# Second layer of a four-layer block on Trainium2: input projections as 256-feature jobs, halves of x summed by VectorE

## The chip, the cores and the metric

The kernel runs on one core of one Trainium2 chip. The metric is the device time of one execution in microseconds (us), median of the runs. In the profile PE is TensorE, PEld its weight loads, DVE VectorE, ACT ScalarE, POOL GpSimd, SP SyncE.

## The reference

Four layers work on x (256 tokens, 2048 features): two of one block, two of another, each with an input projection of x, a mixing part, and an output projection. The change is in the second layer (`odd_layer`), whose core is:

```
proj = rmsnorm(x, norm_g) @ w_in                       # 2048 -> 6160
xc, zc, qd, kd, vd, zd, a_pre, b_pre = split_cols(proj, OD_SIZES)
xconv = causal_dwconv(xc, conv_c_w) + conv_c_b         # 4 taps along the tokens
yc = rg_lru(xconv, gate_w, gate_b, lam) * silu(zc)
q, k, v = split(silu(causal_dwconv(concat([qd, kd, vd]), conv_d_w)), 3)
od = gated_delta_chunkwise(l2norm(q), l2norm(k), v, beta, g)
yd = rmsnorm(od, onorm_g) * silu(zd)
y = concat([yc, yd]) @ w_out
```

Each of xc, zc, qd, kd, vd, zd has 1024 features. `gated_delta_chunkwise` needs the inverse of a lower triangular matrix per head and chunk. Everything is 32-bit floating point.

## The kernel before

**Precision.** Every 32-bit operand of a large product is cut into a high and a low part. ScalarE copies a weight piece to WH (`split`, line 1066), VectorE subtracts it to get WL (line 1432), TensorE forms high times high, high times low and low times high. The transposed x of a layer stands in XHL, for each of 16 k-tiles (128 input features) the high half (256 tokens) beside the low half.

**Jobs and pieces.** The work is a list of jobs (`job_list`), one for each block of output columns, and each job is cut into pieces of 512 KB of weights (`piece_list`). There are 626 pieces; piece p is loaded by SP to a ring of 8, its high part goes to a ring of 6. Three modes: "tok" has tokens on the partitions of the result; "feat" has 512 features in four groups of 128, three products of 256 columns for each group and k-tile (lines 739 to 741), 2 k-tiles to a piece; "wide" has 256 features, 4 k-tiles to a piece, and its product with the high weights takes both halves of x at once, 512 columns (lines 720, 723), with one more of 256 columns for each group with the low weights (lines 721, 722). In wide mode the accumulator (two banks of 512 columns, two accumulators in turns) holds for each group two sums of 256 columns, and whoever reads it has to add them (`halves_of`). The third and fourth layers use wide mode for their rotated inputs, the first and second "feat".

**Order.** Every engine walks through the same pieces. At piece p it does its own part of `split` for piece p + 5, then the read-out of a job that ends with p (`evacuate`), then the steps that `plan` has put at p. `plan` is written by hand: `put(slot, step, item)`. TensorE does piece p and then the small products of the steps of p. TensorE does not start a job before the accumulator of the job before the last is read out. Semaphores alone hold the engines together, and no engine leaves its order.

**The second layer** is pieces 177 to 305. Its jobs run qd 0, kd 0, ab, vd 0, qd 1, kd 1, vd 1 (pieces 177 to 225, with 193 for ab), xc (226 to 241), zd in tok mode (242 to 257), zc (258 to 273), output. A conv job (qd, kd, vd, xc) ends with ScalarE's copy from the accumulator to `conv_ring` (line 1111, two halves of 512), GpSimd's product with the row of 1/rms (line 1955), ScalarE's scaled copy (`copied`, line 1241 or 1243), VectorE's three taps for two groups of 128 features (`taps`, line 1674, six instructions) and ScalarE's `silu` (line 1249). A zc job ends with VectorE's product of accumulator and row (line 1460); `gate_c` is ScalarE's silu (line 1360) and GpSimd's product, `split_c` the high and low part of it (lines 1366, 1859).

Beside that the plan runs the delta rule of 8 heads in two halves. For each half come `delta_a`, `delta_k`, `delta_q` (lines 937 to 950 on TensorE, 1743 to 1763 on VectorE, 1296 to 1298 on ScalarE), the triangular solve `tri` in ten parts (VectorE, lines 1770 to 1795, two columns of 15 in a part; GpSimd clears three tiles ahead of it, lines 2007 to 2009; ScalarE copies its result, line 1315), then `level_x` and `level_y` (blocks of the inverse put together by products, lines 964, 978, 981) and `solve1` to `solve4`. The first `tri` stands at pieces 213 to 224, its `level_x` at 227 and `level_y` at 229; the second at 251 to 260, its `level_x` at 263. The LRU's `scan` (lines 1848 to 1852) stands at 261 to 272.

## Time and profile before

| | |
|---|---|
| median of 3 runs | 1919.39 us (1919.13 to 1920.65) |
| profiled execution: time, span | 1919.7 us, 1917.5 us |
| PE busy | 1908.2 us, 100% of the span |
| PEld busy | 1665.5 us, 87% |
| DVE busy | 1203.8 us, 63% |
| ACT busy | 1016.9 us, 53% |
| POOL busy | 165.0 us, 9% |
| SP's weight queue, share of 16 DMA engines | 52.9% |
| granted TensorE clock, mean | 0.999 |

Busy time is an average over stages with different limits. A matmul's length in the profile takes in its run through the array, so matmuls overlap and the sum of their lengths is more than the time they hold the engine; what one costs is the distance from its start to the start of the next.

### The profile page before, as it was taken

The page shows a single profiled execution, that of the slowest core. Times are in us where ns is not written, and L with a number is a line of the kernel's source. Part 1 is how long each engine was busy: PE and PEld are TensorE (multiplying, and loading weights), DVE is VectorE, ACT ScalarE, POOL GpSimd, SP SyncE. Part 2 cuts the span into 40 slices and gives each one's busy share as a digit, 9 for nine tenths or more (in the row PEclk, how much of TensorE's full clock was granted, in tenths as well). Part 3 has the DMA queues.
Part 4 walks back from the last instruction along what each step waited for, and adds up shares of the span by engine and source line. Part 5 has one row for each costly group of instructions (what it writes and reads, how often), then busy time and mean ns, then how long its engine had stood idle before and what let it go on. Part 6 is the DMA issues. An engine that isn't in the chain of part 4 may idle for free.

```text
span 1917.5 us, 27227 instructions
## 1 busy us (share of the span) xinstructions
PE 1908.2 (100%) x10884; PEld 1665.5 (87%) x10884; DVE 1203.8 (63%) x1672; ACT 1016.9 (53%) x1582; POOL 165.0 (9%) x142
## 2 busy tenths in 40 slices
PE   9999999999999999999999999999999999999998
PEld 9988888888899999898888888888888888888886
DVE  6456554554566776787557888655565778754553
ACT  7345445664557755765543345556554344446643
POOL 0000000110002101200001111000000111100110
PEclk9999999999999999999999999999999999999999
DMA  9555555555554444444565554555555555555453
GB/s 340 177 181 176 165 187 184 173 165 187 180 175 157 156 151 143 161 155 153 181 198 191 191 176 165 180 178 164 176 185 189 187 187 171 162 186 174 161 201 132
DMA packets 95037, 340.32 MB, mean 177 GB/s; under 512 B 10704, under 2 KB 11472, under 8 KB 94784
## 3 DMA queue, kind: packets, MB, share of 16 engines
q1 hardware_dynamic: 93392, 333.76, 52.9%
q0 software_dynamic: 944, 3.61, 0.6%
q8 instruction: 87, 1.43, 0.3%
q10 hardware_dynamic: 576, 1.21, 0.2%
q14 instruction: 38, 0.31, 0.1%
HBM read 336.44 MB, written 2.10 MB: 177 GB/s over the span
## 4 chain that ended last, share of the span: by engine, by line
PE 100%; ACT 0%; DVE 0%; issue 0%
PE ACC L715 18%; PE ACC L717 18%; PE ACC L716 18%; PE ACC L723 6%; PE ACC L720 6%; PE ACC L739 6%; PE ACC L740 5%; PE ACC L741 5%; PE ACC L722 3%; PE ACC L721 3%; PE PM L842 1%; PE PM L857 1%; PE PM L895 1%; PE PM L879 1%; PE PM L880 1%; PE PM L878 1%
## 5 line engine op out<-in xcount | busy, mean ns | idle before, releaser
L1432 DVE TENSOR_TENSOR WL<-RAW,WH 128x1024 fp32r<-128x1024 f32 (+1 forms) x624 | 794.6, 1289 | 545.7 <-ACT WH L1066 544.3
L1066 ACT ACTIVATE WH<-RAW 128x1024 fp32r<-128x1024 f32 (+1 forms) x626 | 651.0, 1052 | 517.6 <-PE ACC L717 279.8
L715 PE MATMUL ACC<-WH,XHL 128*128 128x512 f32 x1024 | 407.1, 398 | 0.0
L717 PE MATMUL ACC<-WH,XHL 128*128 128x512 f32 x1024 | 399.0, 390 | 0.0
L716 PE MATMUL ACC<-WL,XHL 128*128 128x512 f32 x1024 | 398.7, 389 | 0.0
L739 PE MATMUL ACC<-XHL,WH 128*128 128x256 f32 x872 | 249.8, 287 | 0.0
L740 PE MATMUL ACC<-XHL,WH 128*128 128x256 f32 x872 | 246.6, 283 | 0.0
L741 PE MATMUL ACC<-XHL,WL 128*128 128x256 f32 x872 | 246.6, 283 | 0.0
L717 PEld LDWEIGHTS ACC<-WH,XHL 128*128 128x128 f32 x1024 | 192.2, 188 | 40.7
L716 PEld LDWEIGHTS ACC<-WL,XHL 128*128 128x128 f32 x1024 | 192.4, 188 | 38.9
L715 PEld LDWEIGHTS ACC<-WH,XHL 128*128 128x128 f32 x1024 | 192.4, 188 | 38.7
L720 PE MATMUL ACC<-XHL,WH 128*128 128x512 f32 x512 | 205.3, 401 | 0.0
L723 PE MATMUL ACC<-XHL,WH 128*128 128x512 f32 x512 | 202.5, 396 | 0.0
L739 PEld LDWEIGHTS ACC<-XHL,WH 128*128 128x128 f32 x872 | 167.2, 192 | 0.6
L740 PEld LDWEIGHTS ACC<-XHL,WH 128*128 128x128 f32 x872 | 167.2, 192 | 0.2
L741 PEld LDWEIGHTS ACC<-XHL,WL 128*128 128x128 f32 x872 | 167.2, 192 | 0.0
L722 PE MATMUL ACC<-XHL,WL 128*128 128x256 f32 x512 | 142.5, 278 | 0.0
L721 PE MATMUL ACC<-XHL,WL 128*128 128x256 f32 x512 | 142.1, 277 | 0.0
L722 PEld LDWEIGHTS ACC<-XHL,WL 128*128 128x128 f32 x512 | 96.1, 188 | 23.4
L721 PEld LDWEIGHTS ACC<-XHL,WL 128*128 128x128 f32 x512 | 96.3, 188 | 21.8
L1960 POOL TENSOR_TENSOR S<-S 128x512 f32<-128x512 f32 x32 | 66.9, 2092 | 479.6 <-DVE S L1480 479.6
L715 PE MATMUL ACC<-WH,YHB 128*128 128x512 f32 x256 | 100.9, 394 | 0.0
(365 smaller groups left out, 2428.3 us busy)
## 6 DMA issues: line engine op xcount, KB each, us to landing
RAW<-in_w SPq DMA_DIRECT2D x621, 512.0 KB, 3.3
X<-in_x SPq DMA_DIRECT2D x4, 512.0 KB, 10.0
RAW<-in_w SPq DMA_DIRECT2D x6, 256.0 KB, 4.3
Y<-in_xT SPq DMA_DIRECT2D x2, 512.0 KB, 11.2
S<-in_bias POOLq DMA_DIRECT2D x8, 128.0 KB, 2.3
S<-in_od_gate_w POOLq DMA_DIRECT2D x1, 1024.0 KB, 5.9
S<-in_final_norm POOLq DMA_DIRECT2D x1, 1024.0 KB, 7.3
out<-Y SPq DMA_DIRECT2D x2, 512.0 KB, 2.6
```

What stands on the lines that cost most here:

```text
L715: e.matmul(o, th, hi[:, kk, :], start=f, stop=False)
L716: e.matmul(o, th, lo[:, kk, :], start=False, stop=False)
L717: m = e.matmul(o, tl, hi[:, kk, :], start=False, stop=l)
L720: e.matmul(acc[0], wh0, XHL3[:, kt, :], start=f, stop=False, skip_group_check=True)
L721: e.matmul(acc[0][:, 0:256], wl0, xh, start=False, stop=l, skip_group_check=True)
L722: e.matmul(acc[1][:, 0:256], wl1, xh, start=f, stop=False, skip_group_check=True)
L723: m = e.matmul(acc[1], wh1, XHL3[:, kt, :], start=False, stop=l, skip_group_check=True)
L739: e.matmul(o, wh, xh, start=f and g % 2 == 0, stop=False, skip_group_check=True)
L740: e.matmul(o, wh, xl, start=False, stop=False, skip_group_check=True)
L741: m = e.matmul(o, wl, xh, start=False, stop=l, skip_group_check=True)
L1066: e.activation(hi, src, ACT.Copy).then_inc(s_hi)
L1432: e.tensor_tensor(lo, src, hi.bitcast(F32), ALU.subtract).then_inc(s_lo)
```

## The change

The conv jobs and the zc jobs of the second layer go from "feat" with 512 features to "wide" with 256: 8 conv jobs become 16, 2 zc jobs become 4, over the same 80 pieces. The read-out of a conv job is now one `tensor_reduce` of VectorE that adds the halves (1024 columns to 512), where ScalarE copied two times 512. That of a zc job is such a reduction and a product with the row. The plan's slots for `copied`, `taps` and `silu` follow the new jobs, one slot each behind the last piece of a job (they were spread over four slots behind the larger one). `gate_c` and `split_c` are put at new slots. The transposes `xt` of the second layer's x come one piece earlier behind an output job.

```diff
 EVAC = {...
-        "conv": (2, 0), "zc": (0, 2), "add": (0, 2), "rope": (0, 4)}
+        "conv": (0, 1), "zc": (0, 2), "add": (0, 2), "rope": (0, 4)}
...
-    def wide(layer, name, w, c0, kind):
+    def wide(layer, name, w, c0, kind, part=(0, 1, 2, 3)):
-        for i in range(4):
+        for i in part:
             jobs.append(Job(layer, name, i, w, c0 + 256 * i, 256, "wide", kind, (0, 1, 2, 3)))
...
         for name, c0 in (("qd", 2048), ("kd", 3072), ("vd", 4096)):
-            jobs.append(Job(1, name, b, w, c0 + 512 * b, 512, "feat", "conv", (0, 1, 2, 3)))
+            wide(1, name, w, c0, "conv", (2 * b, 2 * b + 1))
...
-    both(1, "xc", w, 0, "feat", "conv")
+    wide(1, "xc", w, 0, "conv")
     both(1, "zd", w, 5120, "tok", "zd")
-    both(1, "zc", w, 1024, "feat", "zc")
+    wide(1, "zc", w, 1024, "zc")
...
-                    put(L(layer, "out", q // 2) + 2, "xt", 8 * (layer + 1) + q, 1)
+                    put(L(layer, "out", q // 2) + (1 if layer == 0 else 2), "xt", 8 * (layer + 1) + q, 1)
...
-            for c in range(8):
+            for c, (name, b) in enumerate(CONV):
                 for i in range(2):
-                    put(L(1, *CONV[c]) + 1 + i, "copied", (c, i))
-                    put(L(1, *CONV[c]) + 2 + 2 * i, "taps", (c, i))
+                    last = L(1, name, 2 * b + i)
+                    put(last + 1, "copied", (c, i))
+                    put(last + 2, "taps", (c, i))
                     if c < 6:
-                        put(L(1, *CONV[c]) + 3 + 2 * i, "silu", (c, i))
+                        put(last + 3, "silu", (c, i))
...
-                    put((b1 + 92, L(1, "zc", 1) + 1)[b] + i, "gate_c", (b, i))
-                    put((b1 + 93, L(1, "zc", 1) + 2)[b] + i, "split_c", (b, i))
+                    at = L(1, "zc", 2 * b + i) + ((5, 3), (2, 1))[b][i]
+                    put(at, "gate_c", (b, i))
+                    put(at + 1 + (b == 0), "split_c", (b, i))
...
# ScalarE
-                elif J.kind == "conv":
-                    k = CONV.index((J.name, J.b))
-                    e.wait_ge(s_mm, p + 1)
-                    if k > 1:
-                        e.wait_ge(s_tap, 12 * (k - 1))
-                    for i in range(2):
-                        e.activation(conv_ring(k, i), acc[i], ACT.Copy).then_inc(s_evA)
...
# VectorE
+                elif J.kind == "conv":
+                    c, i = CONV.index((J.name, J.b // 2)), J.b % 2
+                    e.wait_ge(s_mm, p + 1)
+                    if c > 1:
+                        e.wait_ge(s_tap, 12 * c + 6 * i - 18)
+                    e.tensor_reduce(two(conv_ring(c, i)), halves_of(j), AX, ALU.add).then_inc(s_evD)
                 elif J.kind == "zc":
+                    z = two(ZC[:, 512 * (J.b % 2):512 * (J.b % 2) + 512])
                     e.wait_ge(s_mm, p + 1)
-                    if J.b:
-                        e.wait_ge(s_zg, 2)
-                    for i in range(2):
-                        e.tensor_tensor(two(ZC[:, 512 * i:512 * i + 512]), two(acc[i]), row2, ALU.mult).then_inc(s_evD)
+                    if J.b > 1:
+                        e.wait_ge(s_zg, J.b - 1)
+                    e.tensor_reduce(z, halves_of(j), AX, ALU.add).then_inc(s_evD)
+                    e.wait_ge(s_evD, D_AT[j] - 1)
+                    e.tensor_tensor(z, z, row2, ALU.mult).then_inc(s_evD)
...
# GpSimd
                 elif J.kind == "conv":
-                    k = CONV.index((J.name, J.b))
+                    x = two(conv_ring(CONV.index((J.name, J.b // 2)), J.b % 2))
                     e.wait_ge(s_row, 2)
-                    for i in range(2):
-                        x = two(conv_ring(k, i))
-                        e.wait_ge(s_evA, A_AT[j] - 1 + i)
-                        e.tensor_tensor(x, x, row2, ALU.mult).then_inc(s_cx)
+                    e.wait_ge(s_evD, D_AT[j])
+                    e.tensor_tensor(x, x, row2, ALU.mult).then_inc(s_cx)
```

Three places of the order, where the prediction has its terms. VectorE at pieces 212 and 213, the start of the first triangular solve (L1432 is the weight split, L1674 a tap, L1770 the first step of `tri`), before:

```order
L1763 SCALAR_TENSOR_TENSOR S<-PM,SM,SC 128x128
L1432 TENSOR_TENSOR WL<-RAW,WH 128x1024 x2
L1674 SCALAR_TENSOR_TENSOR S<-S,VC 128x255 x2
L1674 SCALAR_TENSOR_TENSOR S<-S,VC 128x254 x2
L1674 SCALAR_TENSOR_TENSOR S<-S,VC 128x253 x2
L1770 STREAM_TRANSPOSE SC<-SC 128x256
```

and of the change (L1427 is the weight split, L1455 the new reduction, L1677 a tap, L1773 and L1783 belong to `tri`):

```order
L1766 SCALAR_TENSOR_TENSOR S<-PM,SM,SC 128x128
L1427 TENSOR_TENSOR WL<-RAW,WH 128x1024 x2
L1455 TENSOR_REDUCE S<-ACC 128x512
L1773 STREAM_TRANSPOSE SC<-SC 128x256
L1775 TENSOR_TENSOR SC<-SC,VC 128x256
L1777 TENSOR_TENSOR SC<-SC 128x128
L1778 COPY SC<-VC 128x128
L1427 TENSOR_TENSOR WL<-RAW,WH 128x1024
L1783 STREAM_SHUFFLE SC<-SC 128x8
```

The six taps ahead of the solve have gone to piece 215, inside it, and a reduction stands in their place; two more reductions (pieces 217 and 221) stand inside the solve.

ScalarE at pieces 206 to 209 (L1066 is the weight split, L1249 `silu`, L1296 to L1298 the exponentials of `delta_a`, L1111 the conv read-out), before:

```order
L1066 ACTIVATE WH<-RAW 128x1024
L1249 ACT_TABLE_LOAD
L1249 ACTIVATE S<-S 128x256 x2
L1066 ACTIVATE WH<-RAW 128x1024
L1296 ACT_TABLE_LOAD
L1296 ACTIVATE SC<-PM,SM 128x128
L1297 ACTIVATE SC<-SC,SM 128x128
L1298 ACTIVATE SC<-SC,SM 128x128
L1066 ACTIVATE WH<-RAW 128x1024 x2
L1111 ACTIVATE S<-ACC 128x512 x2
L1296 ACTIVATE SC<-PM,SM 128x128
```

and of the change (L1068 is the weight split, L1236 `copied`, L1244 `silu`, L1291 to L1293 the exponentials):

```order
L1068 ACTIVATE WH<-RAW 128x1024
L1236 ACTIVATE S<-S,VC 128x256 x2
L1068 ACTIVATE WH<-RAW 128x1024
L1291 ACTIVATE SC<-PM,SM 128x128
L1292 ACTIVATE SC<-SC,SM 128x128
L1293 ACTIVATE SC<-SC,SM 128x128
L1068 ACTIVATE WH<-RAW 128x1024
L1244 ACT_TABLE_LOAD
L1244 ACTIVATE S<-S 128x256 x2
L1068 ACTIVATE WH<-RAW 128x1024
L1291 ACT_TABLE_LOAD
L1291 ACTIVATE SC<-PM,SM 128x128
```

The `silu` with its table load has moved from piece 206 to 208, and the exponential's table load from 207 to 209.

VectorE at pieces 260 and 261, the end of the second solve (L1789 to L1795 its last part, L1848 to L1852 a scan), before:

```order
L1789 TENSOR_TENSOR SC<-SC,VC 128x256
L1791 STREAM_TRANSPOSE SC<-SC 128x256
L1795 COPY SC<-SC 32x8x32 x4
L1432 TENSOR_TENSOR WL<-RAW,WH 128x1024
L1848 SCALAR_TENSOR_TENSOR Y<-S,Y 128x256
L1850 TENSOR_TENSOR S<-S,Y 128x256
L1852 SCALAR_TENSOR_TENSOR Y<-S 128x256
L1432 TENSOR_TENSOR WL<-RAW,WH 128x1024 x2
```

and of the change (L1461 is the reduction of the first zc job, L1463 its product with the row, L1851 to L1855 a scan):

```order
L1792 TENSOR_TENSOR SC<-SC,VC 128x256
L1794 STREAM_TRANSPOSE SC<-SC 128x256
L1798 COPY SC<-SC 32x8x32 x4
L1427 TENSOR_TENSOR WL<-RAW,WH 128x1024
L1461 TENSOR_REDUCE ZC<-ACC 128x512
L1463 TENSOR_TENSOR ZC<-ZC,C 128x512
L1851 SCALAR_TENSOR_TENSOR Y<-S,Y 128x256
L1853 TENSOR_TENSOR S<-S,Y 128x256
L1855 SCALAR_TENSOR_TENSOR Y<-S 128x256
L1427 TENSOR_TENSOR WL<-RAW,WH 128x1024 x2
```

The read-out of a zc job, which came first at piece 265, comes first at piece 261, ahead of the scan.

## Rows read from the trace of the kernel before

**Rows 1.** The page: span, busy time, granted clock by slice, chain

```profile
span 1917.5 us, 27227 instructions
PE 1908.2 (100%) x10884; PEld 1665.5 (87%) x10884; DVE 1203.8 (63%) x1672; ACT 1016.9 (53%) x1582; POOL 165.0 (9%) x142
...
PEclk9999999999999999999999999999999999999999
...
PE 100%; ACT 0%; DVE 0%; issue 0%
```

**Rows 2.** Timeline of TensorE, feature mode: start us, us, engine, line, operation

```profile
541.13 0.28 PE L739 MATMUL ACC<-XHL,WH 128*128 128x256 f32 x1
...
542.57 0.28 PE L739 MATMUL ACC<-XHL,WH 128*128 128x256 f32 x1
```

**Rows 3.** Timeline of TensorE, wide mode, third layer

```profile
1016.09 0.39 PE L720 MATMUL ACC<-XHL,WH 128*128 128x512 f32 x1
...
1016.79 0.40 PE L720 MATMUL ACC<-XHL,WH 128*128 128x512 f32 x1
```

**Rows 4.** Timeline of TensorE: first two products behind a small job, both modes

```profile
700.35 0.36 PE L739 MATMUL ACC<-XHL,WH 128*128 128x256 f32 x1
700.56 0.28 PE L740 MATMUL ACC<-XHL,WH 128*128 128x256 f32 x1
...
1105.73 0.58 PE L720 MATMUL ACC<-XHL,WH 128*128 128x512 f32 x1
1106.15 0.28 PE L721 MATMUL ACC<-XHL,WL 128*128 128x256 f32 x1
```

**Rows 5.** Four lines: count, ns shortest/median/longest, first to last start

```profile
L1472 DVE TENSOR_REDUCE S<-ACC x32: 1216/1224/1225, 1021.9 to 1673.3; 128x512 f32<-128x1024 f32 x32
L1111 ACT ACTIVATE S<-ACC x16: 582/592/598, 557.9 to 752.9; 128x512 f32<-128x512 f32 x16
L1460 DVE TENSOR_TENSOR ZC<-ACC,C x4: 680/682/691, 841.1 to 869.8; 128x512 f32<-128x512 f32 x4
L1955 POOL TENSOR_TENSOR S<-S,C x16: 1273/1298/2245, 558.7 to 754.4; 128x512 f32<-128x512 f32 x16
```

**Rows 6.** Windows of VectorE: us, busy (count), granted clock, DMA share, GB/s

```profile
650.20:692.90 42.70, 40.96 (x113) 1.00 0.52 173
833.60:880.80 47.20, 45.29 (x75) 1.00 0.45 146
```

**Rows 7.** Timeline of VectorE, inside the first triangular solve

```profile
667.04 0.21 DVE L1782 TENSOR_TENSOR SC<-SC 128x48 f32<-128x48 f32 x1
667.28 1.30 DVE L1784 TENSOR_TENSOR SC<-SC 128x48 f32<-128x48 f32 x1
```

**Rows 8.** Timeline of ScalarE, ahead of that solve and behind it

```profile
633.21 1.28 ACT L1249 ACT_TABLE_LOAD   x1
...
691.22 1.73 ACT L1315 ACTIVATE SC<-SC 32x256 f32<-32x256 f32 x4 [3.27 <-DVE SC L1789]
...
701.05 1.09 ACT L1325 ACTIVATE SC<-PM 128x512 f32<-128x512 f32 x2
```

**Rows 9.** Timeline of TensorE: `level_x` behind piece 227, `level_y` behind piece 229

```profile
698.57 2.03 PE L964 MATMUL PM<-SC,S 128*128 128x128 f32 x16
...
706.19 0.39 PE L978 MATMUL PM<-SC 128*128 128x128 f32 x2
```

**Rows 10.** Timeline of GpSimd, the same stretch

```profile
655.97 0.95 POOL L2009 MEMSET S<- 128x1024 f32 x1
667.22 2.55 POOL L1955 TENSOR_TENSOR S<-S,C 128x512 f32<-128x512 f32 x2 [10.30 <-ACT S L1111]
```

**Rows 11.** Timeline of VectorE, then of TensorE, end of the zc jobs

```profile
870.42 0.73 DVE L1802 TENSOR_TENSOR SC<-SC,PM 64x256 f32<-64x256 f32 x2
...
876.47 0.75 DVE L1859 TENSOR_TENSOR YLA<-Y,YHA 128x512 fp32r<-128x512 f32 x1
...
874.07 1.05 PE L992 MATMUL PM<-S,SC 128*128 128x128 f32 x8
```

More of the change, by code:

```diff
@@ L1358, in gate_c @@
                 z = ZC[:, 512 * i:512 * i + 512]
-                e.wait_ge(s_evD, at_D(1, "zc", b) - 1 + i)
+                e.wait_ge(s_evD, at_D(1, "zc", 2 * b + i))
                 e.activation(z, z, ACT.Silu).then_inc(s_zs)
```

## The prediction

> **What bounds the kernel now.** I read the page first. The chain that ended last is TensorE for 100% of the span, and TensorE is busy for 1908.2 of 1917.5 us at a granted clock of 2.4 GHz in every slice [rows 1]. So a change pays only if TensorE gets the same sums from less time, and it costs whatever makes TensorE wait, which today nothing does. Next come the timelines of TensorE in the two modes. In feature mode two products L739 that lie twelve products apart start at 541.13 and 542.57 [rows 2]: 1.44 us for one k-tile of 512 features, a piece of two k-tiles 2.88 us. In wide mode four products start 0.70 us apart (1016.09 to 1016.79, [rows 3]; a whole piece of four takes 2.787), so 1.394 us for a k-tile of 512 features. Last I looked at who feeds TensorE. VectorE is only 63% busy over the span, but not evenly: in 650.2 to 692.9, the first triangular solve, it works 40.96 of 42.7 us, and in 833.6 to 880.8, the zc jobs with the scans, 45.29 of 47.2 [rows 6]. There it is a second bound, held off TensorE by slack alone.
>
> **The sum, against the profiled execution (1919.7 us; the median of 1919.39 lies 0.3 below it).**
>
> *Products.* 80 pieces change mode, 64 of conv and 16 of zc. Each loses 2.880 - 2.787 = 0.093 us: **-7.5 us**.
>
> The Trainium skill, "TensorE: Matmul & The Clock Gate", Part 1, speaks against a gain of this size: it puts back-to-back products at N / 2.4 GHz + 2.5 ns. By that rule, twelve products of 256 columns take 1.310 us and the wide mode's eight 1.300, so that 160 k-tiles would give 1.7 us and not 7.5. The trace does not agree: it has 120 ns for a product of 256 columns in feature mode [rows 2], and the two timelines decide the term.
>
> *Behind the small products.* The first product behind a small job holds TensorE longer: 0.21 us in place of 0.12 in feature mode, 0.42 in place of 0.235 in wide mode [rows 4]. Thus 0.09 against 0.185 more. Some 25 pieces here follow such a job; behind the deltas feature mode also pays 0.19. I count 0.1 us for 10 of them: **+1.0 us**, between 0 and 2.4.
>
> *Read-outs.* Each conv reduction costs VectorE 1.22 us by the same instruction of the third layer (L1472), 1.15 from start to start. ScalarE loses 16 copies of 0.59 us (L1111), and GpSimd keeps its 16 products of 1.3 us (L1955) [rows 5]. A zc job of 256 features costs VectorE 1.15 + 0.6, where 512 features cost 1.2 in two (L1460) [rows 5]. Where VectorE has air (pieces 177 to 205 and 229 to 250) this hides behind TensorE, which is fed five pieces ahead; without that cover each would cost its full 1.15. The transposes `xt` come one piece earlier and wait for two short additions of VectorE that have that piece's time less; I price them at nothing. The weight transfers keep size, order and ring.
>
> *First solve.* I followed VectorE's queue from piece 205 on with the lengths of before. It enters the solve late by 2.6 us: `silu` with its table load of 1.28 us [rows 8] now stands at piece 208, ahead of the split that VectorE awaits (1.4), and the reduction at 209 costs 1.2. Inside stand three reductions (213, 217, 221), +3.5. The sets of taps between 211 and 223 stay four. At 214 ScalarE's scaled copy now waits for reduction and GpSimd, and GpSimd's three clears of 0.96 us [rows 10] stand behind its product, where they used to stand free. ScalarE's mask copies wait for them, and with them the next split: VectorE idles 2.9 us. So the solve's last copy ends 9.0 us later than now. Today it ends at 691.22 + 1.73 = 692.95 [rows 8], and TensorE takes it up at 698.57 [rows 9], a margin of 5.6. TensorE comes there 2.2 us earlier (27 pieces by 0.093, less 0.3 behind small jobs). The wait is 9.0 + 2.2 - 5.6 = **+5.6 us**. Queued behind TensorE's wait is the whole weight stream; part of it may show earlier, at pieces 222 to 226, as a wait for the split, the read-out or the squares of the norms. It is the same delay once.
>
> *Turn behind it.* `level_y` needs ScalarE's copies of `level_x`. The first of them ends near 701.6 [rows 8], 4.6 us before it is used at 706.19 [rows 9]. Now ScalarE has, behind the late solve, three splits, the wait for a reduction and for GpSimd, a scaled copy and a table load. I get 9.1 us from solve to copy, against 7.6 in which TensorE gets there: a wait between 0 and 1.5, **+1.0 us**.
>
> *Second solve and zc.* VectorE's queue from 833.6 on is full [rows 6] and gets 4 x 1.15 us of reductions (the products with the row stay four times 0.6) and a low-part subtraction (L1859, 0.6) that moves ahead, less 0.5 us of air: 4.7 later. `solve1` starts at 874.07 on a result that VectorE has at 871.15 [rows 11], a margin of 2.9; TensorE comes 1.2 earlier (16 pieces, less 0.3). **+3.0 us**; a wait at the second `level_x` of about half a microsecond, which has no margin left today, is part of this.
>
> Sum: -7.5 + 1.0 + 5.6 + 1.0 + 3.0 = **+3.1 us**, so 1919.4 + 3.1 = 1922.5 us. A measurement here tells a change from no change at about 0.2%, 3.84 us, that is below 1915.6 or above 1923.2. **Forecast: no change that can be told**, since nearly all of the gain on TensorE comes back as waits for VectorE.
>
> **Rivals.**
>
> *Faster: the waits stay small.* My ledger has links of ScalarE and GpSimd in it (the 2.9 us of idle, the late table load) that the trace of before does not show in this arrangement; if they fall away, the first wait is about 2.5, and if VectorE meets the zc stretch with air, the second is near nothing. Then -7.5 + 1.0 + 2.5 = -4.0, 1915.4; with no wait at all 1912.9. For it speaks that all conv steps now follow their jobs sooner; against it that VectorE's busy share in the first solve is 96% before anything is added [rows 6]. Chance 0.20.
>
> *Slower: GpSimd's products hold VectorE up inside the solve.* A VectorE product of 48 columns took 1.30 us, beginning with GpSimd's product at 667.22, where its neighbour of the same size took 0.21 [rows 7, 10]. Before, one pair of GpSimd products falls in the solve; now three single ones do, each with its own start. Each can add 1.1 us to the same late chain, and the mark of 1923.2 is passed if the first one does (0.7 us is missing). With two to three of them the sum is +5.3 to +6.4, 1925.2.
>
> The Trainium skill, "SBUF — State Buffer", states the rule behind such a row: VectorE with two SBUF inputs and GpSimd share a port pair as an exclusive lock, and the loser blocks for a whole instruction. The trace agrees in that one row.
>
> Chance 0.38, the upper end of my ledger included.
>
> *It does not do what it says.* If products of the wide mode in this layer start no closer than those of feature mode, -7.5 falls away, and with the waits shrunk by it (TensorE 3.7 us later in all at the two places) the time is 1926. Against it stands that weights, x and accumulators are of the same shape in the third layer [rows 3]. Chance 0.03, taken with the slower side. The rule of the Trainium skill's page on the clock gate, quoted above, comes out near this case.
>
> **How the numbers follow.** No change 0.42, slower 0.38 with the case just named, faster 0.20. The first case alone spans 1917 to 1923.2. The range should leave out 2 in 10: it reaches down to 1914.0, which leaves out the case with no wait at all, and up to 1927.0, three hold-ups by GpSimd and 2.4 behind small jobs.
>
> **What would show it.** TensorE's timeline: pieces 185 to 192 take 2.79 us each; behind piece 227, or in pieces 222 to 227 before it, idle time of 4 to 7 us, released by ScalarE's last copy of the solve, by a weight split or a reduction; about 1 us before the first `level_y`; some 3 us between the second `level_x` and `solve1`. Windows: VectorE 24 to 25 us busier between the starts of the second and third layer's jobs, ScalarE some 9 us less. I am wrong if TensorE's idle time in the second layer sums to under 5 us (then faster), or if the solve's copy is more than 11 us later against TensorE than now (then slower). TensorE's granted clock should stay at 2.4 GHz; were it to fall behind the longest wait, that would be a cost that my sum does not have.

## The result, and the profile after

The changed kernel takes 1933.13 us (median of 4 runs, 1932.85 to 1935.03) against 1919.37 for the kernel before (4 runs, 1919.13 to 1920.65): a ratio of 1.0071 with a 95% interval of 1.0060 to 1.0083, 13.8 us slower. The prediction had 1922.5, at most 1927.0, and called it no change that can be told.

The page of the changed kernel, where [rows 1] are those of before: span, busy time of the engines, and the chain that ended last by engine.

```profile
span 1931.1 us, 25972 instructions
PE 1909.5 (99%) x10244; PEld 1633.8 (85%) x10244; DVE 1225.3 (63%) x1692; ACT 1007.6 (52%) x1566; POOL 170.3 (9%) x142
...
PE 89%; DVE 6%; ACT 3%; issue 1%; POOL 1%; ACTq 0%; DVEq 0%; POOLq 0%
```

The engines' busy times moved about as forecast: VectorE +21.5 us (24 to 25 forecast), ScalarE -9.3 (some 9). What is new is the last line. The chain was TensorE alone; now 11% of it lies on other engines. TensorE's busy time is up by 1.3 us although it has 640 products fewer, a first hint that some of them ran slowly.

The waits of TensorE say for what (engine, tile and line that waited, what it waited for, us in total, times, the longest). The wait of 1.5 us for L1486 is at the start of the program and was there before.

```profile
PE PM L966 <- DVE SC L1809: 2.7, 4, 1.1
PE PM L939 <- POOL SC L2000: 2.7, 1, 2.7
PE PM L951 <- DVE S L1760: 2.4, 2, 1.5
PE PM L923 <- ACT S L1269: 2.2, 1, 2.2
PE PM L771 <- DVE S L1486: 1.5, 1, 1.5
PE ACC L722 <- DVE WL L1427: 0.8, 2, 0.5
PE PM L966 <- issue: 0.8, 1, 0.8
PE PM L980 <- ACT SC L1320: 0.5, 1, 0.5
PE PM L994 <- DVE SC L1805: 0.4, 1, 0.4
```

To place them I took the start of every piece's first product in both traces and subtracted. The shift is how much later than before TensorE begins the piece; it was +0.6 at piece 173 already, a difference of the start.

| piece | shift at its start, us | it takes longer by | waits in it |
|---|---|---|---|
| 203 | -1.58 | +2.91 | `delta_a` L939 for GpSimd's diagonals L2000 |
| 209, 211 | +0.93, +1.99 | +1.12, +1.65 | `delta` L951 for VectorE |
| 222, 224 | +2.86, +3.43 | +0.54, +0.43 | products for weight splits |
| 226 | +3.88 | +2.80 | norms L923 for ScalarE's squares L1269 |
| 227 | +6.68 | +2.62 | none; the clock is low |
| 229 | +9.22 | +0.69 | `level_y` L980 |
| 258 | +8.94 | | |
| 263, 267, 271 | +8.47, +8.69, +9.68 | +0.46, +1.24, +1.85 | `level_x` L966 for VectorE |
| 272 | +11.53 | +1.48 | none; the clock is low |
| 275 | +12.96 | +0.63 | `solve1` L994 |
| 276 | +13.59 | | unchanged from here on |

Between these entries nearly every piece of a conv or zc job is shorter by 0.07 to 0.10 us, as forecast, and those of zd (242 to 257), which are the same in both kernels, take the same time. In wide mode two products L722 start 0.70 us apart in this layer too (timeline of TensorE), and four products are one k-tile of 256 features, as in [rows 3]. Below them is the first wait.

```profile
615.13 0.39 PE L722 MATMUL ACC<-XHL,WH 128*128 128x512 f32 x1
...
615.83 0.40 PE L722 MATMUL ACC<-XHL,WH 128*128 128x512 f32 x1
...
619.41 0.70 PE L939 MATMUL PM<-SC,C 128*128 128x256 f32 x2 [2.72 <-POOL SC L2000]
```

It can be followed backwards by the timelines of GpSimd, VectorE and ScalarE (start, length, operation; in brackets the idle time before and what ended it).

```profile
600.20 2.14 POOL L1956 TENSOR_TENSOR S<-S,C 128x512 f32<-128x512 f32 x1 [15.30 <-DVE S L1455]
615.82 2.11 POOL L1956 TENSOR_TENSOR S<-S,C 128x512 f32<-128x512 f32 x1 [13.47 <-DVE S L1455]
617.89 2.90 POOL L2000 TENSOR_TENSOR SC<-C,SM 128x128 f32<-128x128 f32 x8
```

```profile
598.84 1.22 DVE L1455 TENSOR_REDUCE S<-ACC 128x512 f32<-128x1024 f32 x1
599.98 1.21 DVE L1427 TENSOR_TENSOR WL<-RAW,WH 128x1024 fp32r<-128x1024 f32 x1
606.73 1.23 DVE L1427 TENSOR_TENSOR WL<-RAW,WH 128x1024 fp32r<-128x1024 f32 x1 [5.53 <-ACT WH L1068]
...
614.46 1.22 DVE L1455 TENSOR_REDUCE S<-ACC 128x512 f32<-128x1024 f32 x1
```

```profile
602.38 0.91 ACT L1236 ACTIVATE S<-S,VC 128x256 f32<-128x256 f32 x2 [3.76 <-POOL S L1956]
...
617.96 0.91 ACT L1236 ACTIVATE S<-S,VC 128x256 f32<-128x256 f32 x2 [3.40 <-POOL S L1956]
```

The sum for the job that ended with piece 197 begins at 598.84, GpSimd's product follows at 600.20, and ScalarE, whose scaled copy L1236 stands one piece behind the job in its queue, has stood idle for 3.76 us when the product is done. The weight copy L1068 that VectorE needs is queued behind the scaled copy and the squares, so VectorE stands idle for 5.53 us, and the next sum comes at 614.46. GpSimd can then start its product only at 615.82, and the diagonals, queued behind it, at 617.89. In the kernel before ScalarE read the accumulator itself and went on with other work while GpSimd multiplied. The waits of ScalarE give the total, first in the kernel before, then in the changed one (both scaled copies, L1236 and L1238):

```profile
ACT S L1241 <- POOL S L1955: 0.5, 1, 0.5
```

```profile
ACT S L1236 <- POOL S L1956: 35.9, 10, 5.1
ACT S L1238 <- POOL S L1956: 7.6, 3, 3.2
```

From 0.5 us to 43.5 us, on an engine that feeds VectorE, which feeds TensorE.

The two pieces without a wait are explained by windows (us, then each engine's busy time and count, the granted clock, DMA share and GB/s):

```profile
699.00:706.50 7.50, 7.50 (x32) 6.73 (x32) 6.50 (x18) 3.44 (x8) 0.00 (x0) 0.55 0.00 1
706.50:716.00 9.50, 8.98 (x61) 8.00 (x62) 4.33 (x4) 5.71 (x12) 2.14 (x1) 1.00 0.34 111
...
873.70:877.20 3.50, 3.50 (x13) 2.93 (x12) 3.43 (x5) 2.02 (x3) 1.95 (x1) 0.51 0.00 0
```

Behind the wait of 2.2 us at piece 226, and behind those at 271, the mean granted clock was 0.55 and 0.51, so that TensorE ran at 1.2 GHz for most of the 7.5 us of the one window and for nearly all of the 3.5 us of the other. Behind the wait of 2.7 us at 619.41 it did not fall in this execution.

### The profile page after: what moved, and what is told of

Same layout as the page of the kernel before. It is cut to its first block, busy times and chain, and to the rows that moved or that the text cites. A ratio compares the mean times of both kernels' runs of the same rounds, so it can differ in the third digit from the quotient of the medians.

```text
span 1931.1 us, 25972 instructions
## 1 busy us (share of the span) xinstructions
PE 1909.5 (99%) x10244; PEld 1633.8 (85%) x10244; DVE 1225.3 (63%) x1692; ACT 1007.6 (52%) x1566; POOL 170.3 (9%) x142
## 4 chain that ended last, share of the span: by engine, by line
PE 89%; DVE 6%; ACT 3%; issue 1%; POOL 1%; ACTq 0%; DVEq 0%; POOLq 0%
PE ACC L717 18%; PE ACC L719 18%; PE ACC L718 18%; PE ACC L722 8%; PE ACC L725 8%; PE ACC L724 4%; PE ACC L723 4%; DVE WL L1427 2%; PE ACC L741 1%; PE ACC L742 1%; PE ACC L743 1%; ACT WH L1068 1%; PE PM L844 1%; DVE S L1677 1%; PE PM L859 1%
## 5 line engine op out<-in xcount | busy, mean ns | idle before, releaser
L1427 DVE TENSOR_TENSOR WL<-RAW,WH 128x1024 fp32r<-128x1024 f32 (+1 forms) x624 | 792.7, 1286 | 546.0 <-ACT WH L1068 544.9
L1068 ACT ACTIVATE WH<-RAW 128x1024 fp32r<-128x1024 f32 (+1 forms) x626 | 649.6, 1052 | 494.0 <-PE ACC L719 278.3
L722 PE MATMUL ACC<-XHL,WH 128*128 128x512 f32 x832 | 336.6, 405 | 0.8 <-DVE WL L1427 0.8
L725 PE MATMUL ACC<-XHL,WH 128*128 128x512 f32 x832 | 330.6, 397 | 0.0
L724 PE MATMUL ACC<-XHL,WL 128*128 128x256 f32 x832 | 232.4, 279 | 0.0
L723 PE MATMUL ACC<-XHL,WL 128*128 128x256 f32 x832 | 231.9, 279 | 0.0
L724 PEld LDWEIGHTS ACC<-XHL,WL 128*128 128x128 f32 x832 | 157.2, 189 | 38.3
L723 PEld LDWEIGHTS ACC<-XHL,WL 128*128 128x128 f32 x832 | 157.5, 189 | 34.7
L722 PEld LDWEIGHTS ACC<-XHL,WH 128*128 128x128 f32 x832 | 158.7, 191 | 2.6 <-DVE WL L1427 1.5
L725 PEld LDWEIGHTS ACC<-XHL,WH 128*128 128x128 f32 x832 | 156.8, 189 | 0.0
L719 PE MATMUL ACC<-WH,YLB 128*128 128x512 f32 x256 | 99.8, 390 | 0.0
L718 PE MATMUL ACC<-WL,YHB 128*128 128x512 f32 x256 | 99.6, 389 | 0.0
L717 PE MATMUL ACC<-WH,YHA 128*128 128x512 f32 x240 | 94.6, 394 | 0.0
L719 PE MATMUL ACC<-WH,YLA 128*128 128x512 f32 x240 | 93.5, 390 | 0.0
```

The costliest lines, as they stand in the source:

```text
L717: e.matmul(o, th, hi[:, kk, :], start=f, stop=False)
L718: e.matmul(o, th, lo[:, kk, :], start=False, stop=False)
L719: m = e.matmul(o, tl, hi[:, kk, :], start=False, stop=l)
L722: e.matmul(acc[0], wh0, XHL3[:, kt, :], start=f, stop=False, skip_group_check=True)
L723: e.matmul(acc[0][:, 0:256], wl0, xh, start=False, stop=l, skip_group_check=True)
L724: e.matmul(acc[1][:, 0:256], wl1, xh, start=f, stop=False, skip_group_check=True)
```

## Experiments

Fourteen kernels ran, each beside the kernel before on the same chip. Differences are from the median of before that was taken with it (1919.5 to 1919.8). Statements about single pieces are from the same subtraction of traces as above. Kernels that mix the modes have more code, so their line numbers are higher by some 15 to 40.

### Which jobs cost what

Each kernel puts only some of the layer's jobs in wide mode, with the change's slots for them, and leaves the rest as before:

```
for c, (name, b) in enumerate(CONV):
    wide(...) or Job(1, name, b, w, c0 + 512 * b, 512, "feat", "conv", ...)
s1: qd, kd, vd    s2: qd, kd, vd of the first half    s3: xc    s4: zc
```

> Only the twelve wide jobs of qd, kd and vd (48 pieces, their reductions on VectorE, their steps one, two and three pieces behind the job); xc and zc stay as before. Theory A (the cost sits where the traces of before and after differ: the wait for GpSimd's diagonals at piece 203, 2.9 us, the deltas at 209 and 211, 2.8, the norms and the first level_x at 226 and 227, 5.4 with the low clock, then level_y 0.7, weight splits 1.0, less 48 x 0.09 = 4.3): about +8 to +9 us, 1927 to 1929, and nothing wrong from piece 229 on. Rival B (the harm comes mostly from the zc stretch and the xc jobs, whose VectorE work runs into the second solve, as it would if only total work on VectorE counted): under +4 us.

> Only the first half of qd, kd, vd wide (six jobs, pieces 177 to 201 without the small one, 24 pieces); everything from piece 202 on as before. Theory A: the conv steps of these jobs stand in a tight chain VectorE, GpSimd, ScalarE, VectorE, so that GpSimd's diagonals are late at piece 203 even here: gain 24 x 0.09 = 2.2, the wait at 203 of about 2.9 again, sum 0 to +1. Rival (my ledger's view: these pieces have air, the reductions hide): -2 us, 1917.3, no wait at 203.

> Only the four xc jobs wide (16 pieces, 226 to 241). In the traces TensorE's shift fell by 0.4 us between pieces 229 and 257, less than 16 x 0.09 = 1.5. Theory A: with the rest as before, this stretch has air for VectorE: -1 to -1.5 us, 1918.0, unless the first reduction at 229 hits level_y. Rival: VectorE's four extra reductions just behind the first solve push the triangular work of the second solve and cost 1 us or more: 1920.5.

> Only the four zc jobs wide (16 pieces, 258 to 273). Theory A: cost at the second solve as in the trace of after (263 +0.5, 267 +1.2, 271 +1.9, 272 +1.5 with the low clock, 275 +0.6, less 1.2): about +4 us, 1923.5. Rival: the second solve was late in after only because VectorE came into it late from the earlier stages; then alone it costs under +1.5 us, and the four parts sum to less than the whole change's +13.7.

Measured: qd, kd, vd wide 1928.61 (+9.1; ratio 1.0051, 1.0038 to 1.0063); their first half 1921.19 (+1.7; 0.9999 to 1.0016); xc 1918.36 (-1.2; 0.9985 to 1.0003); zc 1925.85 (+6.3; 1.0033, 1.0021 to 1.0045). The three disjoint parts, 9.1, -1.2 and 6.3, sum to 14.3 where the whole change has 13.8: the losses nearly add, and there are two of them. The intervals of the first half and of xc both include 1, so what is said of those two rests on their traces. The zc part alone does not lose in quite the same places as inside the change: 7.3 us at 263, 267, 271, 275 and 276, the last 1.6 at a low clock, where the change has 5.7 at 263 to 275.

The xc jobs show the gain bare: pieces 226 to 241 are 1.3 us shorter in all, and TensorE waits nowhere. The first half of qd, kd and vd shows the loss nearest to bare. TensorE was 2.7 us ahead at piece 203 (0.6 of it from the start), waited there for GpSimd's diagonals again, and the next piece was 1.50 us longer without a wait. Its timeline:

```profile
618.19 0.73 PE L955 MATMUL PM<-SC,C 128*128 128x256 f32 x2 [2.58 <-POOL SC L2036]
...
619.78 0.41 PE L759 MATMUL ACC<-XHL,WL 128*128 128x256 f32 x1
620.00 0.41 PE L757 MATMUL ACC<-XHL,WH 128*128 128x256 f32 x1
...
622.50 0.28 PE L758 MATMUL ACC<-XHL,WH 128*128 128x256 f32 x1
622.62 0.28 PE L759 MATMUL ACC<-XHL,WL 128*128 128x256 f32 x1
```

L757, L758 and L759 follow one another every 0.21 to 0.22 us until about 622.1 and every 0.12 from then on. The rival of s2, that these pieces have air and hide everything, fell; the theory's 0 to +1 was passed by the low clock, which it did not have. The zc part cost more than I expected (6.3, not 4). Its waits, and the VectorE queue at the last of them:

```profile
PE PM L983 <- DVE SC L1833: 2.7, 4, 1.0
PE PM L1011 <- DVE SC L1829: 2.0, 1, 2.0
```

```profile
876.64 1.22 DVE L1485 TENSOR_REDUCE ZC<-ACC 128x512 f32<-128x1024 f32 x1
877.90 0.69 DVE L1487 TENSOR_TENSOR ZC<-ZC,C 128x512 f32<-128x512 f32 x1
878.50 0.74 DVE L1829 TENSOR_TENSOR SC<-SC,PM 64x256 f32<-64x256 f32 x2
```

The sum and product of the last zc job stand directly ahead of the subtraction that `solve1` waits for: 1.9 us from start to start, where before the read-out took 1.2.

### Order, clock, handshake or step distance

All four start from the changed kernel. e3 leaves out the scaling of the conv inputs by the row of 1/rms, so its results are not those of the reference.

```
e1  - put(b1 + diag[i], "diag", (half, i))
    + put(b1 + diag[i] - (half == 0), "diag", (half, i))
e2  + e.matmul(o[:, 0:256], XH3[:, 0, 0:128], XH3[:, 0, :], start=True, stop=True)   # n times
      ahead of the waits in norm_sum (second half, part 0) and level_x (second half)
e3  - e.tensor_tensor(x, x, row2, ALU.mult).then_inc(s_cx)        # GpSimd, conv
      copied:  - e.wait_ge(s_cx, ...)    + e.wait_ge(s_evD, at_D(...))
e4  - put(last + 1, "copied", ...); put(last + 2, "taps", ...); put(last + 3, "silu", ...)
    + put(last + 2, "copied", ...); put(last + 3, "taps", ...); put(last + 4, "silu", ...)
```

> The changed kernel with GpSimd's diagonals of the first half one piece earlier (200 and 201), so that they stand ahead of its product for the job that ends with piece 201. Theory A (order on GpSimd): the wait of 2.7 us before the first delta_a at piece 203 goes, the deltas at 209 and 211 and all behind may shift by the same amount or lose it: 1929 to 1931. Rival (VectorE is the bound there, the diagonals only the messenger): the wait moves to the deltas behind and the time stays 1933.

> The changed kernel with idle time of TensorE filled by products whose results nobody reads: 17 of 128x256 (2.0 us) before the norms' wait at piece 226, and 2, 6, 9 and 5 before the four waits of the second half's level_x. The waits themselves stay. Theory C (the granted clock falls to 1.2 GHz because TensorE stood idle, and that is a cost beside the waits): the granted clock stays 1.00 through 699 to 706 and 873 to 877, piece 227 is 2.3 us or so shorter and piece 272 1.5: 1929 to 1930. Rival D (the drop has another cause, for instance the small fp32 products of the solves or the load of the whole chip, or work of the other engines makes these pieces long): same clock trace and 1933 or more.

> The changed kernel without GpSimd's product with the row of x's norms (it leaves that scaling of the conv inputs out); ScalarE's scaled copy waits for VectorE's sum directly. Theory B (the harm in the conv part comes from the handshake VectorE, GpSimd, ScalarE, VectorE): the wait at 203 goes (2.9), the deltas and norms lose most of theirs: -5 to -9 us, 1924 to 1928, ScalarE's idle time before its scaled copies falls from 3 us and more to about 1. Rival A2 (VectorE's own added work is the bound; GpSimd only rides along): only the wait at 203 goes, -3 us, 1930.

> The changed kernel with each job's scaled copy, taps and silu one piece later (two, three and four pieces behind the job). Theory B: ScalarE and VectorE no longer stand and wait for GpSimd's product, so what they feed (weight splits, diagonals) is on time: -2 to -5 us, 1928 to 1931. Rival A2: nothing is won, since VectorE works the same in total, and norms and solves come later by a piece in places: 1932 to 1936.

Measured: e1 1932.54 (+12.9), e2 1932.48 (+12.8), e3 1923.82 (+4.2, 1921.81 to 1924.38), e4 1923.35 (+3.7, 1921.18 to 1926.09), against +13.8 for the change.

**e4** is the answer for the conv part: with three steps per job one piece later, nothing removed, 10 of the 13.8 us are gone. That was more than either theory had: Theory B had -2 to -5. The waits of ScalarE in e4:

```profile
ACT S L1236 <- POOL S L1956: 6.1, 5, 2.8
ACT S L1238 <- POOL S L1956: 0.9, 1, 0.9
```

43.5 us have become 7.0. VectorE is busy for 1226.4 us in e4 and 1225.3 in the change, so the amount of VectorE's work alone is not what cost 10 us. TensorE's waits that are left in e4's conv part are 0.5 us at piece 203 and 1.3 at 227; it is 3.3 us ahead of before at piece 258 and loses 4.7 in the zc stretch, as the change does. (The trace is of e4's fastest execution, 1921.2 us.)

What e4 moved can be seen in VectorE's queue: the start of the first solve, ahead of it the six taps, and the solve's last transpose; the changed kernel first, then e4, then the kernel before.

```profile
656.87 2.46 DVE L1677 SCALAR_TENSOR_TENSOR S<-S,VC 128x255 f32<-128x255 f32 x6
659.24 0.35 DVE L1755 SCALAR_TENSOR_TENSOR SC<-PM,SM,SC 128x128 f32<-128x128 f32 x1
...
664.07 0.45 DVE L1773 STREAM_TRANSPOSE SC<-SC 128x256 f32<-128x256 f32 x1
...
704.02 0.45 DVE L1794 STREAM_TRANSPOSE SC<-SC 128x256 f32<-128x256 f32 x1
```

```profile
654.69 0.45 DVE L1773 STREAM_TRANSPOSE SC<-SC 128x256 f32<-128x256 f32 x1 [0.22 <-ACT SC L1300]
...
694.34 0.45 DVE L1794 STREAM_TRANSPOSE SC<-SC 128x256 f32<-128x256 f32 x1
```

```profile
658.67 0.44 DVE L1770 STREAM_TRANSPOSE SC<-SC 128x256 f32<-128x256 f32 x1
...
691.22 0.45 DVE L1791 STREAM_TRANSPOSE SC<-SC 128x256 f32<-128x256 f32 x1
```

The table sets these times against the start of TensorE's piece 213.

| us | before | change | e4 | e3 | g2 (below) |
|---|---|---|---|---|---|
| piece 213 starts | 651.4 | 655.0 | 648.8 | 651.0 | 648.6 |
| first transpose behind it | 7.3 | 9.1 | 5.9 | 9.1 | 5.8 |
| first to last transpose | 32.6 | 40.0 | 39.7 | 35.6 | 37.5 |

In e4 the solve is as long as in the change and begins 3.3 us earlier: taps that stood directly ahead of the delta steps (L1755 to L1760, on which TensorE waits at pieces 209 and 211) now stand behind them, and those waits are gone.

**e3** has nearly the same total by another way. The wait at 203 is gone and piece 209 is longer by only 0.3 us, but piece 211 is longer by 1.7 as in the change, and the solve begins as late. What is shorter is the solve, by 4.4 us: without GpSimd's products VectorE's L1775 and L1785 in it are not held up (the last section has the numbers). So e3 does not show that the hand-over through GpSimd cost all 10 us; it shows that the solve's late start costs little once the solve itself is shorter.

**e1** shows that moving one late step alone moves the wait: TensorE no longer waits at 203 but at 207, for the deltas (L951, which waits 3.6 us in place of 2.4 in all), and the piece behind it is 1.5 us longer at a granted clock of 0.63 (633.0 to 637.6).

**e2** is a miss that teaches. Most of the idle time is filled, and in the two windows where the clock had fallen it stays up. But it falls in the window between, behind a wait of 1.0 us that is left before `level_x` at 705.74:

```profile
699.00:706.50 7.50, 6.53 (x50) 6.12 (x50) 6.39 (x18) 3.44 (x8) 0.00 (x0) 1.00 0.22 73
706.50:716.00 9.50, 8.53 (x45) 7.47 (x44) 4.45 (x4) 5.71 (x12) 2.13 (x1) 0.82 0.17 59
...
873.70:877.20 3.50, 3.50 (x21) 3.10 (x21) 3.43 (x5) 2.63 (x5) 1.53 (x1) 1.00 0.00 0
```

and hardly anything is won. By these windows TensorE spent about 6.8 us at 1.2 GHz in the change and about 3.4 in e2 behind piece 226; from 226 to 242 it loses 5.1 us in both. So half of that low clock could be taken away for nothing: TensorE met the next wait earlier. What the other half cost is not shown. In the zc stretch piece 272 is 1.5 us shorter, but 275 is longer by 0.7, since `solve1` waits longer for VectorE (1.1 in place of 0.4), and 271 by 0.6, which is the filling's own doing: with the useless products ahead of them, its two `level_x` parts begin 0.5 and 0.6 us later in the piece. The clock explains where much of the time lay in the changed kernel; that it is not most of the cost is likely from this, and not settled.

### Repairs, and a control

```
f1  all conv jobs wide, zc as before, conv steps one piece later (as e4)
f2  f1, diagonals of the first half one piece earlier, and for the job that ends with piece 221:
    taps at last + 4, silu at last + 5
f3  only zc wide (as s4), its product with the row on GpSimd:
    vector   - e.tensor_tensor(z, z, row2, ALU.mult).then_inc(s_evD)
    gpsimd   + e.wait_ge(s_evD, D_AT[j]); e.tensor_tensor(z, z, row2, ALU.mult).then_inc(s_cz)
f4  the kernel before with its conv steps one piece later
```

> All sixteen conv jobs wide with their steps one piece later, zc as before. In the run with the later steps TensorE stood 3.3 us ahead of the kernel before at piece 258 (start-up difference of 0.3 among it), and lost 4.7 in the zc stretch. Theory (the zc loss is a thing of its own and needs nothing from the conv part): 1916.5, between 1915.8 and 1917.3, faster than before. Rival (VectorE carries the conv jobs' work into the second solve): a wait at level_x or solve1 of the second half, 1918 to 1920.

> The same with two more steps moved: GpSimd's diagonals of the first half one piece earlier (0.5 us of wait at piece 203 with the later steps), and the taps and silu of the job that ends with piece 221 one more piece later, so that 2.4 us of taps stand behind the last triangular step of the first half on VectorE and not ahead of it (1.3 us of wait at piece 227). Theory: both waits go, 1914.5 to 1915.5. Rival: the product with the taps is then late for the split behind it, and only the 0.5 is won: 1916.

> Only zc wide (the run that took 6.3 us more), but the product of its sum with the row goes from VectorE to GpSimd: VectorE gets 4 x 0.6 us less. Theory (VectorE's own work is the bound in the zc stretch, a different kind of loss from the conv part): 2 to 4 us of the 6.3 come back, 1922 to 1924. Rival (there too the order of steps or the handshake is what costs): no gain, or a loss from GpSimd's products of 1.3 to 2.1 us in the chain to ScalarE's gate, 1925 to 1928.

> Control: the kernel before, all in feature mode, with its conv steps one piece later as well. Theory (one piece more only repairs what the change did to the steps' distance): 1919.4 within 0.5 us, or slightly worse. Rival (later steps are better for either kernel, so the 9.8 us have nothing to do with the change): 1915 or less.

Measured: f1 1919.17 (-0.6; 0.9986 to 1.0004), f2 1919.40 (-0.4), f3 1921.49 (+1.7; 1.0000 to 1.0018), f4 1919.89 (+0.1; 0.9992 to 1.0010).

**f4**: later steps do nothing for the kernel before. The distance is a matter of the new read-out. **f3**: 2.8 us less work on VectorE (four products of 0.69) takes 4.6 us off zc's loss, so what stands in VectorE's queue binds there, and some of it was low clock (0.89 from 876 to 882 in s4, 1.00 in f3). Whether the amount counts, or that it stood directly ahead of what TensorE awaits, f3 does not tell apart: it changes both. **f1** has the zc stretch exactly as before (3.07 us ahead at piece 258 and at 276), so the conv part does not reach into it. But its times, 1916.5 expected, fell in two groups: 1916.7 to 1917.7 in five executions, 1919.9 to 1920.5 in five others, one between. The mean granted clock was 0.998 to 0.999 in the first group and 0.997 in the second; the trace is of one in the first, 1916.7. **f2** (1914.5 to 1915.5 expected) removed both waits it aimed at and got a new one:

```profile
PE PM L997 <- ACT SC L1344: 3.3, 1, 3.3
```

The silu that I had put later now stood in ScalarE's queue ahead of the copies that `level_y` needs, and itself waited for the taps. In ScalarE's timeline (the copies L1344 begin at 704.09):

```profile
699.62 0.81 ACT L1268 ACTIVATE S<-S 128x256 f32<-128x256 f32 x2 [4.49 <-DVE S L1707]
```

### The clock by itself, and a version that beats both

```
g1  f1, in level_x of the first half:
    + for _ in range(10): e.matmul(bank(bs[0])[:, 0:256], XH3[:, 0, 0:128], XH3[:, 0, :], ...)
      e.wait_ge(s_am, 4 * half + 4)
g2  f2, with silu of the job that ends with piece 221 at last + 8
```

> The version with all conv jobs wide, steps one piece later and zc as before (its times fell in two groups, near 1917 at a mean granted clock of 0.999 and near 1920.2 at 0.997), with ten products of 128x256 that nobody reads (1.2 us) before the first half's first level_x, where TensorE stood idle for 1.3 us. Theory C (the 3 us between the groups are the low clock that this idle time brings about in some executions): all runs in the lower group, median 1916.5 to 1917.5, mean clock 0.999 in each. Rival D (the groups have another cause): two groups again and a median between 1917 and 1920.

> The version with the diagonals one piece earlier and the taps of the job that ends with piece 221 one more piece later, but its silu now at piece 229, behind ScalarE's copies of level_x and beside the silu of the next job (before it stood ahead of them, waited 4.5 us for the taps, and held level_y up by 3.3 us). Theory: no wait of TensorE over 0.5 us is left in the conv part, -5.5 us of products, +0.5 small: 1914.5 to 1915.5 with no second group, faster than both kernels. Rival: the next link in ScalarE's queue (table loads, the scaled copy at 227) holds level_y up again by 1 us or more: 1916 to 1918.

Measured: g1 1917.05 (1916.50 to 1917.83 in eleven executions, mean clock 0.999 in each; ratio 0.9986, 0.9977 to 0.9994). g2 1914.85 (1914.38 to 1915.68; ratio 0.9975, 0.9965 to 0.9985).

In g1 the second group is gone. With 1.2 us of useless products where TensorE would have stood idle for 1.3 us, the median is 2 us lower than f1's. So the low clock most likely costs this kernel about 3 us (1917.0 against 1920.3, the middles of f1's groups) in about half of its executions. Two things keep it from being shown: no trace of the second group was kept, and g1 ran on another chip than f1 (the medians of before on the two are 1919.77 and 1919.81).

g2 is 5.0 us faster than the kernel before and 18 us faster than the change. Its waits of TensorE, whole:

```profile
PE PM L788 <- DVE S L1516: 1.5, 1, 1.5
PE PM L983 <- DVE SC L1839: 0.3, 1, 0.3
PE PM L983 <- issue: 0.2, 1, 0.2
```

TensorE gains 4.98 us between pieces 177 and 276, of 64 x 0.093 = 5.95 that the products give. All of the change's conv jobs are in it, with their reductions in the first solve. It leaves zc in feature mode, so it is a repair of the conv part and not of the whole change.

## Why the prediction was wrong

**The step that failed first** is the sentence that the read-outs at pieces 177 to 205 hide "behind TensorE, which is fed five pieces ahead", with no term for the diagonals and deltas up to piece 211. It priced a chain of four steps (sum on VectorE, product on GpSimd, scaled copy on ScalarE, taps on VectorE) by busy times. But a queue is in order. ScalarE waited for GpSimd with weight copies queued behind, and the delay came back as a late sum and late diagonals at piece 203. At 211, and in part at 209, the deltas came late behind the taps that the plan had put directly ahead of them; e3, without GpSimd's product, keeps 1.7 us of this at 211, and e4, with the taps later, nothing. That gave 5.7 us at pieces 203, 209 and 211 (2.9, 1.1 and 1.7), in the sum at nothing.

**First solve, +5.6 forecast.** Pieces 222 to 227 give 6.4. The ledger's form held, and its end too: against TensorE's piece 213 the solve begins 1.8 us later than before (forecast 2.6) and ends 9.2 later (forecast 9.0). In between two entries were wrong and made up for each other by luck. VectorE's idle time in the solve grew by 0.9 us and not by 2.9; and GpSimd's products held VectorE up in it, about 2 us more than before, which the sum did not have. Six more taps (2.4 us) stand inside the solve than before. The margin was the turning point: in g2 the reductions and the hold-ups are all there and the solve still ends 3.5 us later against piece 213 than before, but that is inside the margin of 5.6, and the first half's `level_x` waits 0.3 us in all.

**Second solve and zc, +3.0 forecast: the second step that failed.** The mechanism was right (VectorE full, sums ahead of `level_x` and `solve1`), the size not: from piece 258 to 276 TensorE falls back by 4.65 us, and with the products' gain of 1.3 that it makes up for, the loss is about 6. The term set 4.7 us of VectorE work against one margin of 2.9 at `solve1`. In the trace TensorE pays before that, at three places (0.5, 1.2 and 1.9 us at pieces 263, 267 and 271), and again at `solve1` (0.6). That each wait makes VectorE's next operations late in turn is a reading; no run tests it. Some 1.5 us were clock.

**The whole.** Against the forecast of +3.1 the two traces lie 13.6 us apart. Of the 10.5 that are missing, 5.7 are the first step, 3.0 zc, 0.8 the first solve, and 0.6 a difference from before piece 173.

**Right.** *Products*: -7.5; a wide piece takes 2.79. *Behind small products*: +1.0; g2 gains 1.0 less than its 64 pieces should give, 0.4 of it at piece 231, thus about 0.6 (0.7 for 80). *The turn* `level_y`: 0.5 us of wait against 1.0. *The moved `xt`*: piece 177 +0.71, 178 -0.79, nothing.

**The rivals.** GpSimd's products inside the solve do hold VectorE up as the rival says; in the changed kernel, by VectorE's timeline:

```profile
664.55 1.33 DVE L1775 TENSOR_TENSOR SC<-SC,VC 128x256 f32<-128x256 f32 x1
...
680.53 1.33 DVE L1785 TENSOR_TENSOR SC<-SC 128x56 f32<-128x56 f32 x1
```

GpSimd's products begin at 664.30 and 680.50, and a third at 692.65, beside which L1785 takes 1.32 us. They are part of the loss, and not all of it: e3, without them, has a solve shorter by 4.4 us and nearly no wait behind it, while g2, where the two products L1815 take 1.33 us as well, has none either, because its solve begins early enough. So either nearly kept the margin, and the sum should have had both. That the clock might fall behind the longest wait was named, outside the sum. The largest fault was one of search: I looked for a full VectorE (a busy share) and began at piece 205, where the first loss was made in pieces in which VectorE was idle for 5.5 us, waiting for ScalarE.

**Open.** e4 moved three steps together; which one matters most was not tried apart. Why zc's wide jobs still cost 1.7 us with the row product on GpSimd was not followed further, and no run moved zc's sum or the steps around it to another place with the work unchanged, as e4 did for the conv jobs.

## What to carry to other kernels

When a read-out moves to another engine, follow the finished value through every queue that it still has to cross, and put each later step at the distance that the new chain needs: an engine that waits in order stops everything it feeds. Subtract the two traces piece by piece before explaining a difference, and give each part of a change a kernel of its own; here one part had its gain bare, one a loss that a shift of three steps removed, and one a loss for which no order without it was tried. After moving a step to end one wait, look at what it now stands ahead of.

## What the hardware did that I had not expected

- The granted clock of TensorE fell from 2.4 to 1.2 GHz behind waits of only 1.0 to 2.7 us in an otherwise unbroken stream (1.0 in e2, 2.2 in the change, 2.6 in s2), for 3.5 to 7 us, and not each time: not behind the 2.7 us at 619.41 in the change, where s2 had it behind the same wait. The Trainium skill, "TensorE: Matmul & The Clock Gate", Part 1, says that an idle array falls back to the lower clock and that the number of slow products differs from run to run of one kernel; f1's two groups and g1's one (1919.17 and 1917.05 in the median) go with both.
- What a low clock costs depends on what comes next: most likely 3 us in f1, and nothing for the half of it that e2 took away behind piece 226, where other engines bound the pieces behind.
- A VectorE product is held up by a GpSimd product that has just begun: L1785 with 56 columns took 1.33 us at 680.53, 0.03 behind GpSimd's start. In e3, without GpSimd's products, the 15 operations L1785 of the solve take 3.4 us from start to start in all, in the change 5.6.
- GpSimd's product L1956 took 2.14 us at 600.20, begun while VectorE's split of 599.98 ran, and 1.29 where it began alone. The Trainium skill, "SBUF — State Buffer", section "SBUF: two separate sides", has the one that starts first keep the shared ports for its whole instruction. The rows agree: the 0.85 us more are near the 0.99 that were left of the split.
